# First modulation, differences and mix of the trunk made row by row, with the first projection group in steps of those rows

## The reference, cut to what matters

```python
sh1, sc1, gt1, sh2, sc2, gt2 = jnp.split(c_act @ P['ada_w'][l] + P['ada_b'][l], 6, axis=-1)
h = modulate(rms_norm(x, P['norm_mix_g'][l]), sh1, sc1)      # h * (1 + scale) + shift
xx = jnp.concatenate([shift_prev[:, None, :], h[:, :-1]], axis=1) - h
xm = h[None] + xx[None] * P['rwkv_mix'][l][:, None, None, :] # six mixes, s = 0 to 5
rkv = jnp.einsum('sbtc,scd->sbtd', xm[:3], P['rwkv_w_rkv'][l])
```

## Time and profile before

| | us |
|---|---|
| median of three runs | 2112.9 |
| lowest and highest | 2107.7, 2115.88 |
| span of the profiled execution, first to last instruction | 2095.1 |
| TensorE busy | 1874.0 (89% of the span) |
| DVE, ACT busy | 699.6, 506.7 |
| mean granted TensorE clock | 0.942 of full |

### The profile page before, as it was taken

One profiled execution on the slowest core, in us unless ns is written; L12 is line 12 of the kernel. 1 busy time (PEld: TensorE's weight loads), 2 busy tenths in 40 slices (PEclk: granted clock), 3 DMA queues, 4 the chain that ended last, 5 costly groups with the idle time before them and its releaser, 6 DMA issues.

```text
span 2095.1 us, 53480 instructions
## 1 busy us (share of the span) xinstructions
PE 1874.0 (89%) x23724; PEld 1499.0 (72%) x23724; DVE 699.6 (33%) x1834; ACT 506.7 (24%) x1111; POOL 82.4 (4%) x135
## 2 busy tenths in 40 slices
PE   5699997798888879799999899999999997999994
PEld 3476774687777757688888784478666676888883
DVE  3310023456666533411111430211777424111115
ACT  1110112234333211311110120211777513111112
POOL 2000004100000000100000200000000001000001
PEclk9799997899999999899999999998899998999997
DMA  8589734810000019499999988165000166999974
GB/s 310 185 284 296 253 129 155 280 24 14 14 13 14 9 38 318 174 376 364 373 378 371 253 184 201 33 184 131 1 2 2 38 228 231 368 379 375 379 299 153
DMA packets 184120, 409.05 MB, mean 195 GB/s; under 512 B 51318, under 2 KB 121426, under 8 KB 175666
## 3 DMA queue, kind: packets, MB, share of 16 engines
q1 hardware_dynamic: 165122, 353.47, 50.6%
q0 software_dynamic: 11040, 39.85, 5.5%
q10 hardware_dynamic: 7760, 12.79, 1.7%
HBM read 354.60 MB, written 55.68 MB: 196 GB/s over the span
## 4 chain that ended last, share of the span: by engine, by line
PE 74%; DVE 7%; issue 7%; ACT 5%; DMA 4%; DVEq 2%; ACTq 1%; POOL 0%; SPq 0%
PE bank L1716 11%; PE bank L413 8%; PE bank L1711 6%; PE bank L1729 5%; PE bank L1476 4%; PE bank L1735 3%; PE bank L2536 3%; PE bank L2585 2%; PE bank L2637 2%; PE bank L376 2%; PE bank L2674 2%; PE bank L433 1%; PE bank L1704 1%; PE bank L1693 1%; ACT fT L637 1%
## 5 line engine op out<-in xcount | busy, mean ns | idle before, releaser
L413 PE MATMUL bank<-xm,wp 128*128 128x272 f32 x512 | 122.3, 398 | 17.8 <-DVE xm L588 17.8
L413 PEld LDWEIGHTS bank<-xm,wp 128*128 128x128 f32 x512 | 97.1, 192 | 40.3 <-DVE xm L588 18.2
L1711 PE MATMUL bank<-wu,xsT 128*32 128x384 f32 x1056 | 120.9, 494 | 4.1 <-issue 4.1
L1711 PE MATMUL bank<-wg,xsT 128*32 128x384 f32 x1056 | 117.9, 487 | 5.8 <-ACT xsT L1896 5.4
L1716 PE MATMUL bank<-wu,xsT 128*32 128x128 f32 x1056 | 121.4, 276 | 0.0
L1716 PE MATMUL bank<-wg,xsT 128*32 128x128 f32 x1056 | 119.4, 273 | 0.0
L1729 PE MATMUL bank<-wd,actT 128*32 128x384 f32 x1056 | 118.1, 486 | 1.3 <-ACT actT L1909 1.3
L1716 PEld LDWEIGHTS bank<-wu,xsT 128*32 128x32 f32 x1056 | 116.9, 112 | 2.9
L1735 PE MATMUL bank<-wd,actT 128*32 128x256 f32 (+1 forms) x704 | 118.4, 326 | 0.4 <-issue 0.4
L1716 PEld LDWEIGHTS bank<-wg,xsT 128*32 128x32 f32 x1056 | 113.5, 110 | 0.0
L2090 DVE TENSOR_TENSOR act<-bank,act 128x384 f32<-128x384 f32 x32 | 17.8, 558 | 256.5 <-PE bank L1716 256.5
(11 more groups left out here) (579 smaller groups left out, 4265.4 us busy)
## 6 DMA issues: line engine op xcount, KB each, us to landing
wg<-in_moe_w_gate_dram SPq DMA_DIRECT2D x22, 2048.0 KB, 18.6
wu<-in_moe_w_up_dram SPq DMA_DIRECT2D x22, 2048.0 KB, 23.7
wd<-in_moe_w_down_dram SPq DMA_DIRECT2D x22, 2048.0 KB, 19.7
adaw<-in_ada_w_dram SPq DMA_DIRECT2D x43, 1024.0 KB, 7.9
w<-in_moe_w_gate_dram SPq DMA_DIRECT2D x10, 2048.0 KB, 18.9
fT<-in_moe_w_up_dram SPq DMA_DIRECT2D x10, 2048.0 KB, 23.9
gall<-in_moe_w_down_dram SPq DMA_DIRECT2D x10, 2048.0 KB, 19.4
wp<-in_rwkv_w_rkv_dram SPq DMA_DIRECT2D x24, 512.0 KB, 7.0
```

What stands on the lines that cost most here:

```text
L413: mm = pe.matmul(bank[rkv_bank(n)][:, 0:HALF], B.wp[g % WP][:, k, :], B.xm[s][:, k, half(h)], start=k == 0, stop=k == KT - 1)
L1711: mm = pe.matmul(ps[32 * j:32 * j + 32, 0:GW], B.xsT[:, k, 32 * j:32 * j + 32], w[:, k, 0:GW], start=k == 0, stop=k == KT - 1)
```

## The change

Semaphores only renamed or merged (`pool_ident` into `pool_masks`, `kinv_ready` into `lasth_ready`) and the counts shifted with them are left out of the diff below.

- TensorE: products 0 and 1, then turns 0 and 1 directly, into two parts of bank 3 (`ada_turned`); then group 0, k by k, both halves at each k, each k waiting for its row of xm (`xm_first`); only then product 2 (loads u = 8 to 11), half of product 3 (u = 12, 13) and turn 2, and group 1.
- SyncE: the three first `wp` loads stand ahead of u = 8 and 9, and the wait for the first kept block is gone.
- ACT raises `first_scaled` after each row it has scaled.
- DVE: the difference of token 0 (8 elements a row) is made out of coefficient and shift ahead of the rows; then the sample columns with their differences; then, row by row, the 511 differences of the prompt and the mix of the row before, with a drain after each pair.

```diff
+def ada_turned(j):
+    return 256 if j == 1 else 0
...
-            for u in range(4 * ADA_FIRST + 2):
+            for u in range(4 * ADA_FIRST):
+                load_ada(u)
+            for g in range(WP):
+                load_wp(g)
+            for u in range(4 * ADA_FIRST, 4 * ADA_FIRST + 2):
                 load_ada(u)
...
-            sp.wait_ge(S("in_ev"), 11)
-            sp.wait_ge(S("ada_ev"), 1)
             for g in range(24):
-                load_wp(g)
+                if g >= WP:
+                    load_wp(g)
...
-            for j in range(ADA_FIRST + ADA_AHEAD):
+            for j in range(ADA_FIRST):
                 ada_product(j, 0)
                 ada_product(j, 1)
-                if j >= 1:
-                    ada_turn(j - 1)
+            for j in range(ADA_FIRST):
+                ada_turn(j)
...
+            pe.wait_ge(S("w_loaded0"), 16)
+            for k in range(KT):
+                pe.wait_ge(S("xm_first"), k + 1)
+                for h in range(2):
+                    mm = pe.matmul(bank[rkv_bank(h)][:, 0:HALF], B.wp[0][:, k, :], B.xm[0][:, k, half(h)], start=k == 0, stop=k == KT - 1)
+                    if k == KT - 1:
+                        mm.then_inc(S("rkv_mm"), 1)
+            for j in range(ADA_FIRST, ADA_FIRST + ADA_AHEAD):
+                ada_product(j, 0)
+                ada_product(j, 1)
...
-            dve_shift_scale(dve, B, 0, "g_mix0", mod(B, 0, 0), mod(B, 0, 1))
-            dve.drain()
-            h = B.fT
-            dve.wait_ge(S("in_ev"), 11)
-
-            dve.tensor_tensor(B.xx[:, :, 1:SEQ], h[:, :, 0:SEQ - 1], h[:, :, 1:SEQ], ALU.subtract)
-            dve.tensor_scalar(B.xx[:, :, 0:1], h[:, :, 0:1], -1.0, None, ALU.mult)
...
+            dve.scalar_tensor_tensor(out=B.coef[:], in0=scale, scalar=1.0, in1=vec(B, "g_mix0").unsqueeze(2).to_broadcast([128, KT, NC]),
+                                     op0=ALU.add, op1=ALU.mult)
+            dve.drain()
+            dve.tensor_tensor(B.xx[:, :, 0:1], h[:, :, 0:1], B.coef[:, :, 0:1], ALU.mult)
+            dve.drain()
+            dve.scalar_tensor_tensor(out=B.xx[:, :, 0:1], in0=B.xx[:, :, 0:1], scalar=-1.0, in1=shift[:, :, 0:1], op0=ALU.mult, op1=ALU.subtract)
+            dve.drain()
+            dve.nop().then_inc(S("norm_x"), KT)
...
+            for k in range(KT + 1):
+                if k < KT:
+                    dve.wait_ge(S("first_scaled"), k + 1)
+                    dve.tensor_tensor(B.xx[:, k, 1:SEQ], h[:, k, 0:SEQ - 1], h[:, k, 1:SEQ], ALU.subtract)
+                if k:
+                    dve.scalar_tensor_tensor(out=B.xm[0][:, k - 1, :], in0=B.xx[:, k - 1, :], scalar=vec(B, "mix0")[:, k - 1:k],
+                                             in1=h[:, k - 1, :], op0=ALU.mult, op1=ALU.add).then_inc(S("xm_first"), 1)
+                dve.drain()
...
-            for s in range(6):
+            for s in range(1, 6):
```

More of the change, by code:

```diff
@@ L243, in _ @@
             keep(ident[:], [[-1, 128]], 0, 1, ALU.not_equal, 1.0)
-            pool.memset(B.ones[:], 1.0).then_inc(S("pool_ident"), 1)
+            pool.memset(B.ones[:], 1.0).then_inc(S("pool_masks"), 1)
             link(pool.memset(B.low128[:], 1.0))
@@ L313, in _ @@
             sp.wait_ge(S("rkv_mm"), 48 + 8)
-            sp.wait_ge(S("xm_ready"), 6)
+            sp.wait_ge(S("xm_ready"), 5)
             sp.wait_ge(S("ada_ev"), 14)
@@ L342, in _ @@
         def _(pe):
-            pe.wait_ge(S("pool_ident"), 1)
+            pe.wait_ge(S("pool_masks"), 1)
             pe.wait_ge(S("vec_loaded"), 16 * 17)
@@ L382, in ada_turn @@
                 pe.wait_ge(S("ada_rows"), j + 1)
[L383 removed]
+                if j >= ADA_FIRST:
                     pe.wait_ge(S("ada_ev"), j)
                 for i in range(2):
[L386 removed]
+                    at = ada_turned(j) + i * 128
+                    mm = pe.transpose(bank[3][:, at:at + 128], B.adas[j % 2][:, i * 128:i * 128 + 128], ident[:])
                 mm.then_inc(S("ada_tr"), 1)
             pe_norm_sum(pe, B, 0)
[L390 removed]
+            for j in range(ADA_FIRST):
                 ada_product(j, 0)
                 ada_product(j, 1)
[L393 to L394 removed]
+            for j in range(ADA_FIRST):
+                ada_turn(j)
             def key_squares(m):
@@ L401, in key_squares @@
                 mm.then_inc(S("ksum_mm"), 1)
+            pe.wait_ge(S("w_loaded0"), 16)
[8 more added lines that the diff above has]
+                ada_product(j, 1)
             for g in range(24):
                 s = g // KT
[L405 to L408, removed]
+                if g and g % KT == 0:
+                    pe.wait_ge(S("xm_ready"), s)
+                if g:
+                    pe.wait_ge(S(f"w_loaded{g % WP}"), 16 * (g // WP + 1))
+                for h in range(2 if g else 0):
                     n = 2 * g + h
@@ L427, in _ @@
             for s, w, c0, c1 in [(3, B.w1, 0, 64), (4, B.a1, 0, 64), (5, B.g1, 0, 128), (5, B.g1, 128, 160)]:
-                pe.wait_ge(S("xm_ready"), s + 1)
+                pe.wait_ge(S("xm_ready"), s)
                 r0 = 64 if s == 4 else 32 if c0 else 0
@@ L524, in _ @@
                 ins.then_inc(S("in_ev"), 1)
-            dve.wait_ge(S("pool_masks"), 1)
+            dve.wait_ge(S("pool_masks"), 2)
             for h in range(2):
@@ L547, in ada_keep @@
             def ada_keep(j):
-                dve.wait_ge(S("ada_tr"), j + 1)
+                dve.wait_ge(S("ada_tr"), max(j + 1, ADA_FIRST))
                 bias = B.vT[:, 4, 8 * j:8 * j + 8].unsqueeze(2).to_broadcast([128, 8, NC])
-                got = bank[3][:, 0:256].rearrange("p (i q n) -> p q i n", i=2, q=4)[:, :, :, 0:NC]
+                got = bank[3][:, ada_turned(j):ada_turned(j) + 256].rearrange("p (i q n) -> p q i n", i=2, q=4)[:, :, :, 0:NC]
                 for q in range(4):
@@ L562, in _ @@
             dve.drain()
-            dve_shift_scale(dve, B, 0, "g_mix0", mod(B, 0, 0), mod(B, 0, 1))
-            dve.drain()
-            h = B.fT
-            dve.wait_ge(S("in_ev"), 11)
-            dve.tensor_tensor(B.xx[:, :, 1:SEQ], h[:, :, 0:SEQ - 1], h[:, :, 1:SEQ], ALU.subtract)
-            dve.tensor_scalar(B.xx[:, :, 0:1], h[:, :, 0:1], -1.0, None, ALU.mult)
+            h, shift, scale = B.fT, mod(B, 0, 0), mod(B, 0, 1)
             hs = h[:, :, SEQ:T].rearrange("p k (b s) -> p k b s", s=DS)
@@ L572, in _ @@
+            dve.drain()
+            dve.nop().then_inc(S("norm_x"), KT)
+            dve.tensor_tensor(hs, hs, B.coef[:, :, 1:NC].unsqueeze(3).to_broadcast([128, KT, DB, DS]), ALU.mult)
+            dve.drain()
+            dve.tensor_tensor(hs, hs, shift[:, :, 1:NC].unsqueeze(3).to_broadcast([128, KT, DB, DS]), ALU.add)
+            dve.drain()
             dve.tensor_tensor(xs[:, :, :, 1:DS], hs[:, :, :, 0:DS - 1], hs[:, :, :, 1:DS], ALU.subtract)
             dve.tensor_tensor(xs[:, :, :, 0], B.vT[:, 1, 0:64].rearrange("p (b k) -> p k b", k=KT), hs[:, :, :, 0], ALU.subtract)
-            dve.tensor_copy(B.lasth[:, 0, :], h[:, :, SEQ - 1])
@@ L575, in _ @@
-            dve.tensor_copy(B.lasth[:, 1:NC, :].rearrange("p n k -> p k n"), hs[:, :, :, DS - 1]).then_inc(S("lasth_ready"), 1)
+            dve.tensor_copy(B.lasth[:, 1:NC, :].rearrange("p n k -> p k n"), hs[:, :, :, DS - 1])
+            for k in range(KT + 1):
[5 more added lines that the diff above has]
+                                             in1=h[:, k - 1, :], op0=ALU.mult, op1=ALU.add).then_inc(S("xm_first"), 1)
+                dve.drain()
@@ L576, in _ @@
+            dve.nop().then_inc(S("norm_done"), 1)
+            dve.tensor_copy(B.lasth[:, 0, :], h[:, :, SEQ - 1]).then_inc(S("lasth_ready"), 1)
             dve.drain()
             kept = ADA_FIRST
-            for s in range(6):
+            for s in range(1, 6):
                 upto = (ADA_FIRST, ADA_FIRST, ADA_FIRST + ADA_AHEAD + 3, 13, 14, 14)[s]
@@ L596, in _ @@
             dve.drain()
-            dve.reciprocal(B.kinv, B.kinv).then_inc(S("kinv_ready"), 1)
+            dve.reciprocal(B.kinv, B.kinv).then_inc(S("lasth_ready"), 1)
             dve_rwkv(dve, B)
             dve_rest(nc, dve, B, io, out)
-ROOT_AT, SCALED_AT = (1, 3, 5, 8, 10), (2, 4, 6, 7, 9)
+ROOT_AT, SCALED_AT = (1, 2, 4, 7, 9), (0, 3, 5, 6, 8)
 def pe_keep_clock(pe, B, b, n):
@@ L637, in act_scale @@
         ins = act.activation(x, x, ACT.Identity, bias=shift[:, k, 0:1], scale=B.coef[:, k, 0:1])
-    ins.then_inc(S("norm_rt"), 1)
+        if i == 0:
+            ins.then_inc(S("first_scaled"), 1)
+    if i:
+        ins.then_inc(S("norm_rt"), 1)
 def pe_norm_sum(pe, B, n):
@@ L654, in pe_norm_sum @@
     mm.then_inc(S("norm_mm"), 1)
[L657 to L670, removed]
 def dve_norm(dve, B, n, i, gain, shift, scale):
@@ L846, in pe_first @@
             pe.wait_ge(S("factors_loaded1"), 64)
-            pe.wait_ge(S("kinv_ready"), 1)
+            pe.wait_ge(S("lasth_ready"), 2)
         if a >= 1:
```

## The result

The changed kernel is faster, by 0.8% in the first comparison. There its median was 2094.01 us (four runs, 2087.85 to 2101.21) against 2114.36 us before, ratio 0.9922 with a 95% interval of 0.9899 to 0.9945. Two later comparisons of the same two kernels, on two different chips, gave 0.9945 (0.9924 to 0.9966) and 0.9938 (0.9915 to 0.9961). As gains they are 16.5, 11.6 and 13 us; weighted by the widths of the intervals their mean is about 13.5 us, give or take 3 (an estimate from the three). Forecast were 9.4 us and 2103.5 us, with a range of 2098 to 2110.5.

What follows compares the result with a forecast made beforehand. Waits from engine to engine bound group 0, TensorE from group 1 on. Group 0 ending 23.0 us earlier, less 11.9 before group 1, less 1.7 for its slow start, gave 9.4: 2112.9 to 2103.5 us, range 2098 to 2110.5.

Steps and rivals of the forecast that it cites:

- the wait of 11.74: DVE's idling before keep 1, with turn 1 behind product 2; forecast gone with turn 1 behind products 0 and 1.
- Parts 1 and 2: Ahead of the rows: turn 1 done by 40.2, keep 1 at 42.37, ACT starting at 43.30, DVE's first row at 45.0.
- Part 3: DVE's differences and mixes row by row: 1.43 us a pair, last xm row at 56.5, DVE pacing group 0.
- Part 4: Group 0 on TensorE in steps: half clock from 47.0, full by some 50.2, ending at 57.5, 23.0 us earlier.
- rival B: Pauses hold TensorE at 1.2 GHz through group 0: gain only 4.3 us, 2108.6 us; chance 0.15.
- Part 5: Between groups 0 and 1: loads 11, 12, 13 land late, at 63.8, 66.4, 69.0; group 1 ends at 80.7.
- the slow start of group 1: Group 1 behind the late loads: 9.03 us instead of 7.34 at a fallen clock, 1.7 us less gain.
- rival A: Clock back to full by group 1's start, or never falling for long: 11.5 to 12 us gained, 2101; chance 0.2.
- rival C: No wait for loads 11 to 13 behind group 0: gain 19 us, 2094 us; chance 0.03.
- The 17.8 us between the span and the median: Profiled span 2095.1 against median 2112.9 of the kernel before; the 17.8 us between were taken as unchanged.
- SyncE's queue costs nothing: Weight loads moved ahead of loads 8 and 9 on SyncE's queue were forecast off the path.
- Rivals C and D: C: no wait for loads, 2094, chance 0.03. D: three-buffer ring stays empty, each group loses 5.6 us, 2126, chance 0.05.

Runs made afterwards that it cites:

- e3: Changed kernel with product 2 put back ahead of the step-wise group 0; ratio to the kernel before 0.989 (0.986 to 0.9921).
- e10: Changed kernel with product 2 put back ahead of the step-wise group 0, second run; ratio to the kernel before 0.9888 (0.9861 to 0.9915).
- e6: Kernel before with only SyncE's queue of the change; ratio to the kernel before 0.9992 (0.9969 to 1.0015).
- e4: Changed kernel with products 0, 1, 2 and the turns in their old order; ratio to the kernel before 0.9926 (0.9901 to 0.9952).

## Why the prediction was right or wrong

**Right: the structure.** That turn 1 is worth the wait of 11.74; that DVE and not ACT paces the rows; that group 0 ends some 22 us earlier and about half of it goes back between group 0 and group 1; that group 1 is the instant to price. At the end of group 1 the forecast was 9.4; the traces have 90.11 - 80.02 = 10.1, and 10.7 counted from the reciprocal.

**Parts 1 and 2** came within 0.2: ACT's first row started 43.84 - 33.47 = 10.4 after the reciprocal, forecast 43.30 - 32.81 = 10.5, and DVE's first difference 12.0, forecast 12.2.

**Part 3, the rows.** 1.48 a pair instead of 1.43, since the mix starts 0.61 behind its difference and not 0.55. The gap behind a mix, drain and signal, is 0.09, forecast 0.10. Last mix at 57.37 - 33.47 = 23.9 after the reciprocal, forecast 56.5 - 32.81 = 23.7.

**Part 4, the steps, and rival B.** Stretches of the trace after, the last three figures being granted clock, DMA share and GB/s:

```profile
45.00:46.00 1.00, 0.00 (x0) 0.00 (x0) 1.00 (x4) 1.00 (x3) 0.00 (x0) 0.50 0.00 0
...
51.00:52.00 1.00, 1.00 (x4) 0.77 (x3) 1.00 (x2) 0.00 (x0) 0.00 (x0) 0.69 0.00 0
...
54.00:55.00 1.00, 0.78 (x4) 0.31 (x2) 1.00 (x2) 0.00 (x0) 0.00 (x0) 1.00 0.00 0
...
56.00:57.00 1.00, 0.71 (x4) 0.41 (x3) 0.91 (x2) 0.00 (x0) 0.00 (x0) 1.00 0.00 0
...
65.00:66.00 1.00, 0.60 (x8) 0.37 (x12) 0.00 (x0) 0.00 (x0) 0.00 (x0) 0.64 1.02 393
```

Half clock while TensorE idles, back at 51.6, 3.9 after the first step (forecast 50.2, about 3), and full through the pauses between the steps. Rival B is out in all three profiles of the changed kernel. The rule of the Trainium skill behind it (TensorE: Matmul & The Clock Gate, section "A second HAM failure mode: psum-queue depth-cycling"), that short pauses between groups of matmuls can make the clock swing, is not borne out here: in the stretches above in which TensorE was busy 0.78 and 0.71 of a microsecond the granted clock was 1.00.

**Part 5, the loads.** From issues at 59.8, 60.7 and 61.5 the three loads landed in 5.6, 7.2 and 8.9 us, where I had 5.2 at the least for the first (5.3 and 5.4 in the two other profiles of the changed kernel); their distance, 2.6 and 2.4, was nearly as forecast. The last landed at 70.42 (forecast 69.0, of which 0.7 is the later start of this execution). That product 2 behind group 0 is the term is shown by e3 and e10, not only argued.

**The step that failed: the clock behind the loads, and nothing behind it.** This is the term of the sum that was mis-sized. I took 11.6 from the landing of load 13 to the end of group 1, as behind group 12, and 1.7 of it for "the slow start of group 1". It took 80.02 - 70.47 = 9.6, and 9.3 and 9.2 in the two other profiles of the changed kernel. The product of load 13 ran at half clock for nearly all of its 1.85, but group 1 took 7.33 and not 9.03: the clock was back at its start, and the 1.7 were nothing in all three.

```profile
71.00:72.00 1.00, 1.00 (x16) 0.29 (x8) 0.00 (x0) 0.00 (x0) 0.00 (x0) 0.50 0.97 352
72.00:73.00 1.00, 1.00 (x9) 0.68 (x6) 0.28 (x4) 0.00 (x0) 0.00 (x0) 0.95 1.06 352
```

So rival A, at a chance of 0.2, was what happened to the group: I had given its argument (three products of 1.93 with short waits keep TensorE busy from 64 on) and then let one row decide, 48.48 and 51.10 staying at half.

The prediction also put the gain behind group 1 at nothing. But the group behind the late load of group 12 took 9.03 and 9.11 in the two profiles of before and 7.67, 7.56 and 7.75 in the three of the changed kernel:

```profile
191.03 7.67 PE bank L433 x32
```

The waits ahead of it are alike (1.54 and 1.45 before, 1.73 and 1.44 after), and the same group took 9.16 and 7.34 in the two profiles with product 2 first. What decides it is not shown. The first factor products, before and after, show the two terms together:

```profile
L433 PE MATMUL bank<-adaw,w x32: 392/392/443, 310.5 to 317.6; 128*64 128x272 f32 x32
```

```profile
L453 PE MATMUL bank<-adaw,w x32: 392/392/443, 299.2 to 306.4; 128*64 128x272 f32 x32
```

From the reciprocal that is 277.7 before (278.0 in the second profile) and 265.7 after (265.2 and 264.9 in the two others). The change had gained 12.0 to 13.1 us there, 12.6 in the mean, where 9.4 was forecast. With that gain the forecast would have been 2100.3, a ratio of 0.994, and faster by over 0.5% the likelier case instead of 0.34. The two later comparisons gave just this, 11.6 and 13 us.

**The range.** 2100.3 lies inside the range of 2098 to 2110.5, so these terms alone don't explain the first median of 2094.01. The range allowed a median to be off by 3 us. The four executions behind this median lie 13 us apart, the interval of their ratio holds gains from 11.6 to 21.4, and the medians of one kernel differed by 13 us from chip to chip. The remaining 6 us are seen in no stage of a trace and didn't come again in the ratios; their cause stays open, and the spread of four executions is enough for them. That 2094 is also the time of rival C is chance: C wanted no wait for the loads, and the three waits are there.

**The 17.8 us between the span and the median.** There is no such time. The profiled execution after shows 2094.82 - 2093.0 = 1.8 us outside its span, and the second profile of before 2102.11 - 2100.3 = 1.8. The profile of before was thus, by the same 1.8, an execution of about 2096.9 us, 11 us below the fastest of the timed runs of 2107.7 to 2115.88 that it was set beside. This spoiled the forecast of the span (2085.7 against 2093.0) but not that of the time, which was the timed median less 9.4 whatever lies between.

**Part "SyncE's queue costs nothing".** In the changed kernel no row shows it to cost anything. But by the trace it is worth 3.5 where product 2 stands ahead of the turn (e6, and e4 agrees), as loads 10 and 11 no longer wait for DVE. The prediction saw the earlier issue and didn't price it, since its own chain had no use for it.

**Rivals C and D** didn't happen: the three waits are there, and behind group 1 the half products follow without a wait until group 12.

## What to carry to other kernels

When work is pulled ahead of the work that frees a buffer, price the next instant at which the two meet, not the end of the work that was pulled: here 22 us at the end of group 0 were 11 at the start of group 1, and moving one product back ahead of the group, into time in which TensorE idled, gave the other 11. Take the parts of a change apart before believing their sum: the turn alone brought 11.6, everything but the turn 14 (3.5 of it the queue), and all together 11. Don't price a group at a falling or rising clock from one row of the trace when an argument for the other level stands beside it: give both a like chance. Let the range be as wide as a median of few executions spreads. And check that the profiled execution is of the level of the timed ones before setting its span beside their median; a ratio on one chip says more than a level.

## What the runs showed of the hardware

- The level of one kernel differed between three chips by as much as this change brought: medians of 2112.09, 2100.19 and 2098.76 us for the kernel before (25, 17 and 15 runs).
- When TensorE fell idle, the granted clock went to 0.50 after 4.2 us (40.6 to 44.8) and 3.9 us (61.4 to 65.3) in the profile after, but after 1.8 us (42.0 to 43.8) in the profile before and 1.1 us (187.0 to 188.2 of after) behind a burst of 1.07 between two pauses. It came back 3.1 us (71.4 to 74.5 of before) to 6.6 us (65.4 to 72.05 of after, with pauses) after the work began again. One and the same stretch, 7.34 at full clock, took 7.33, 7.67, 8.42, 9.03 or 9.65 by that.
- Steps of 0.92 every 1.48 us kept the full clock, in all three profiles of the changed kernel.
- A load of 1 MB by itself took 5.3, 5.4 and 5.6 us from issue to landing with the DMA engines idle before it (three profiles), and the next ones landed 2.4 to 2.7 us apart.
